# Updates by halves of both token tiles, and first transposes in the tail of the stage before, in a two-block decoder kernel

## What is computed

```python
def first_block(x, ...):
    h = x
    for l in range(DEPTH):
        h = h + 0.5 * swiglu(rmsnorm(h, ffn_pre_norm[l]), ...)
        u = rmsnorm(h, mix_norm[l])
        h = h + (pool_mixer(u, ...) if l < N_A_LAYERS else mla_attention(u, ...))
        h = h + 0.5 * swiglu(rmsnorm(h, ffn_post_norm[l]), ...)
        if l == N_A_LAYERS - 1:
            k_nope, k_rope, v = mla_shared_kv(h, ...)
    return rmsnorm(h, final_norm)

def second_block(x, norm_g, ...):
    h = x
    for l in range(DEPTH):
        g = norm_g[l]
        f = swiglu_2(rms_norm(h, g[0]), ffn1_w_in[l], ffn1_w_out[l])
        h = h + FFN_RES * rms_norm(f, g[1])
        m = even_mixer(rms_norm(h, g[2]), ...) if l % 2 == 0 else odd_mixer(rms_norm(h, g[2]), ...)
        h = h + rms_norm(m, g[3])
        f = swiglu_2(rms_norm(h, g[4]), ffn2_w_in[l], ffn2_w_out[l])
        h = h + FFN_RES * rms_norm(f, g[5])
    return h
```

## Time and profile before

| | us |
|---|---|
| median of 3 runs | 1914.13 (1913.56 to 1914.39) |
| profiled execution | 1913.66 |
| its span, first to last instruction | 1911.9 |
| TensorE busy | 1888.3 (99%) |
| VectorE busy | 1227.6 (64%) |
| ScalarE busy | 945.5 (49%) |
| GpSimd busy | 62.4 (3%) |
| granted TensorE clock, mean | 0.999 |

### The profile page before, as it was taken

One profiled execution on the slowest core, in us unless ns is written; L12 is line 12 of the kernel. 1 busy time (PEld: TensorE's weight loads), 2 busy tenths in 40 slices (PEclk: granted clock), 3 DMA queues, 4 the chain that ended last, 5 costly groups with the idle time before them and its releaser, 6 DMA issues.

```text
span 1911.9 us, 34343 instructions
## 1 busy us (share of the span) xinstructions
PE 1888.3 (99%) x13542; PEld 1755.5 (92%) x13542; DVE 1227.6 (64%) x1645; ACT 945.5 (49%) x1295; POOL 62.4 (3%) x98
## 2 busy tenths in 40 slices
PE   9999999999999999999999999999999999999998
PEld 8999999999998889999999998899999998889997
DVE  6666766675555646665766689666666665876665
ACT  5444544454446645444544458644454446455443
POOL 0000100000001000000100000100000001010000
PEclk9999999999999999999999999999999999999999
DMA  7555355545553145555554442655545553344552
GB/s 284 198 197 198 135 202 197 187 166 201 187 197 130 67 143 189 196 197 198 198 196 185 157 144 96 237 207 192 185 165 201 191 198 124 130 153 168 196 197 99
DMA packets 61361, 338.83 MB, mean 177 GB/s; under 512 B 6960, under 2 KB 7344, under 8 KB 32880
## 3 DMA queue, kind: packets, MB, share of 16 engines
q1 hardware_dynamic: 59328, 330.00, 46.8%
q0 software_dynamic: 1968, 7.93, 1.2%
HBM read 336.85 MB, written 1.05 MB: 177 GB/s over the span
## 4 chain that ended last, share of the span: by engine, by line
PE 92%; DVE 3%; ACT 2%; issue 1%; POOL 1%; DMA 0%; SPq 0%; DVEq 0%; ACTq 0%; POOLq 0%
PE X L1582 56%; PE Y L1582 34%; DVE xl L1084 1%; ACT hiA L563 1%; PE X L1600 1%; DVE loA L1057 0%; ACT xh L609 0%; DVE arena L1370 0%; DMA rawA<-in_wa 0%; PE Y L1979 0%; PE X L1622 0%; PE X L1624 0%; POOL ms_eps L465 0%; POOL rstd L451 0%; DVE xs L1120 0%
## 5 line engine op out<-in xcount | busy, mean ns | idle before, releaser
L1582 PE MATMUL X<-xh,hiA 128*128 128x256 f32 x2592 | 722.4, 279 | 4.6 <-DVE xl L1084 3.0
L1582 PE MATMUL X<-xl,hiA 128*128 128x256 f32 x2592 | 717.6, 277 | 0.0
L1582 PE MATMUL X<-xh,loA 128*128 128x256 f32 x2592 | 717.1, 277 | 0.0
L1057 DVE TENSOR_TENSOR loA<-rawA,hiA 128x2048 fp32r<-128x2048 f32 x220 | 504.0, 2291 | 269.0 <-ACT hiA L563 268.6
L1582 PEld LDWEIGHTS X<-xh,hiA 128*128 128x128 f32 x2592 | 486.8, 188 | 9.1 <-issue 4.7
L1582 PEld LDWEIGHTS X<-xl,hiA 128*128 128x128 f32 x2592 | 487.5, 188 | 0.0
L1582 PEld LDWEIGHTS X<-xh,loA 128*128 128x128 f32 x2592 | 487.2, 188 | 0.0
L563 ACT ACTIVATE hiA<-rawA 128x2048 fp32r<-128x2048 f32 (+1 forms) x234 | 423.7, 1811 | 56.7 <-PE Y L1582 30.5
L1582 PE MATMUL Y<-hiB,act_hl 128*128 128x512 f32 (+1 forms) x880 | 275.8, 346 | 0.0
L1582 PE MATMUL Y<-hiB,act_hh 128*128 128x512 f32 x704 | 275.2, 391 | 0.1
L1582 PE MATMUL Y<-loB,act_hh 128*128 128x512 f32 x704 | 275.0, 391 | 0.0
(11 more groups left out here) (250 smaller groups left out, 2079.7 us busy)
## 6 DMA issues: line engine op xcount, KB each, us to landing
rawA<-in_wa SPq DMA_DIRECT2D x221, 1024.0 KB, 5.4
rawB<-in_wb SPq DMA_DIRECT2D x181, 512.0 KB, 3.5
row_gain<-in_rows POOLq DMA_DIRECT2D x8, 512.0 KB, 6.4
arena<-in_gla POOLq DMA_DIRECT2D x1, 1280.0 KB, 10.2
h<-in_x SPq DMA_DIRECT2D x2, 512.0 KB, 4.0
out<-h SPq DMA_DIRECT2D x2, 512.0 KB, 2.6
arena<-in_pool POOLq DMA_DIRECT2D x1, 768.0 KB, 5.6
arena<-in_taps POOLq DMA_DIRECT2D x1, 576.0 KB, 4.5
```

What stands on the lines that cost most here:

```text
L1057: nc.vector.tensor_tensor(loA[p][:, :], rawA[p][:, :], hiA[p][:, :].bitcast(f32), ALU.subtract).then_inc(a_lo, 1)
L1582: return say(nc.tensor.matmul(*args, **kw))
```

## The change

For the stages behind a second-block update (hyb, ffn5, ffn6, gla, ffn7: `crossed`) the update before them adds both first halves first: (0,0), (1,0), (0,1), (1,1). `wait_h` counts places in that order, and `residual` transposes slots 0 to 2 of both tiles and then slots 3 to 7 of both, by calling `transposes` four times with a range of slots. The last update, ahead of the output, stays tile by tile, with `add(0, 1)` ahead of `weighted(1, 0)`.

For mla and ffn3 (`early`) the transposes of tile 0 are issued by the stage before, ahead of its last quarter (`following`), and only tile 1 is left at the start. As nothing but a `mm` releases the owed weight buffer there, ScalarE of ffn3 splits tile a+1 behind `xt_hi`, in two halves with the square of tile 1 between them and that of tile 0 ahead of `xt_hi`; VectorE follows with `half_A`.

The tail of every feed-forward stage gives (1,0) before it finishes the other tile's product for (1,1). The first projection of mla runs over slots with the `xh` products of both tiles, waiting for `xh_done`, and then the `xl` products. `opened` is False for every stage, so `opening` and `block_late` are not used.

```diff
--- before.py
+++ after.py
@@ -62,7 +62,12 @@
         raw = late or kind in ("mla", "gla")
         mixers = [p["kind"] for p in plan if p["kind"] != "final"]
         ahead = bool(mixers) and mixers[-1] == "ffn"
-        s = dict(at, kind=kind, i=i, name=name, second=second, reuse=reuse, late=late, raw=raw, ahead=ahead)
+        before = plan[-1] if plan else None
+        crossed = bool(before) and before["second"]
+        early = raw and bool(before) and not crossed and before["kind"] in ("ffn", "mla")
+        opened = False
+        s = dict(at, kind=kind, i=i, name=name, second=second, reuse=reuse, late=late, raw=raw, ahead=ahead,
+                 crossed=crossed, early=early, opened=opened)
         pre = 0 if reuse else 2
         mid = {"kv": 2, "mla": 2, "hyb": 2, "gla": 8}.get(kind, 0)
         s["norm_mid"] = at["norm"] + pre
@@ -270,7 +275,7 @@
         ident_loaded, zero_set, gain_loaded = sem("ident_loaded"), sem("zero_set"), sem("gain_loaded")
         phase_loaded = {k: sem(f"{k}_loaded") for k in ("pool", "mla", "hyb", "gla")}
         row_loaded = [sem("row_loaded0"), sem("row_loaded1")]
-        half_set = sem("half_set")
+        half_set, half_hi, half_lo = sem("half_set"), sem("half_hi"), sem("half_lo")
         ms_done, eps_done, rstd_done = sem("ms_done"), sem("eps_done"), sem("rstd_done")
         ln_eps = sem("ln_eps")
         sum_eps = sem("sum_eps")
@@ -365,7 +370,8 @@
             if s["update"] == 0:
                 engine.wait_ge(x_loaded[t], 16)
             else:
-                engine.wait_ge(h_done, 4 * (s["update"] - 1) + 2 * t + half + 1)
+                place = 2 * half + t if s["crossed"] else 2 * t + half
+                engine.wait_ge(h_done, 4 * (s["update"] - 1) + place + 1)
 
         HALF = [slice(0, 512), slice(512, 1024)]
         HEAD_AFTER = (0, 3, 5, 7)
@@ -637,16 +643,27 @@
                     act.wait_ge(gain_loaded, 16)
                 if s["reuse"]:
                     latent_square()
-                if a and not s["ahead"]:
+                def token_square(t):
+                    mean_square(s["norm"] + t, h[:, t, :], xs[:, t, :], D ** -0.5)
+
+                halved = s["early"] and not s["ahead"]
+                if halved:
+                    wait_h(act, s, 0)
+                    token_square(0)
+                elif a and not s["ahead"]:
                     split_A(a + 1, (a + 1) % 2)
                 if not s["reuse"]:
                     xt_hi(s, s["name"])
                 if a == 0:
                     split_A(1, 1, 0).then_inc(head_hi, 1)
                     split_A(1, 1, 1)
-                if s["late"]:
-                    for t in range(TT):
-                        mean_square(s["norm"] + t, h[:, t, :], xs[:, t, :], D ** -0.5)
+                if halved:
+                    split_A(a + 1, (a + 1) % 2, 0).then_inc(half_hi, 1)
+                    token_square(1)
+                    split_A(a + 1, (a + 1) % 2, 1)
+                elif s["late"]:
+                    token_square(0)
+                    token_square(1)
                 split_B(b, b % 2)
 
                 def step(f, p, first=False, last=False):
@@ -1057,6 +1074,11 @@
                 nc.vector.tensor_tensor(loA[p][:, :], rawA[p][:, :], hiA[p][:, :].bitcast(f32),
                                         ALU.subtract).then_inc(a_lo, 1)
 
+            def half_A(n, part, done):
+                p, cut = n % 2, slice(D * part, D * part + D)
+                nc.vector.tensor_tensor(loA[p][:, cut], rawA[p][:, cut], hiA[p][:, cut].bitcast(f32),
+                                        ALU.subtract).then_inc(done, 1)
+
             def split_B(n, p):
                 dve.wait_ge(b_hi, n + 1)
                 nc.vector.tensor_tensor(loB[p][:, :], rawB[p][:, :], hiB[p][:, :].bitcast(f32),
@@ -1130,10 +1152,13 @@
                 weighted(0, 0)
                 weighted(0, 1)
                 add(0, 0)
+                if s is plan[-1]:
+                    add(0, 1)
                 weighted(1, 0)
-                add(0, 1)
                 weighted(1, 1)
                 add(1, 0)
+                if s is not plan[-1]:
+                    add(0, 1)
                 add(1, 1)
 
             def ffn(s):
@@ -1142,7 +1167,18 @@
                     latent_keys()
                 else:
                     xt_lo(s, s["name"])
-                if a == 0:
+                halved = s["early"] and not s["ahead"]
+                if s["opened"]:
+                    add_eps(s["norm"], s["square"] + 1, halves=False)
+                if halved:
+                    dve.wait_ge(half_hi, 1)
+                    half_A(a + 1, 0, half_lo)
+                if s["opened"]:
+                    add_eps(s["norm"] + 1, s["square"] + 2, halves=False)
+                if halved:
+                    dve.wait_ge(a_hi, a + 2)
+                    half_A(a + 1, 1, a_lo)
+                elif a == 0:
                     dve.wait_ge(head_hi, 4)
                     nc.vector.tensor_tensor(loA[1][:, 0:D], rawA[1][:, 0:D], hiA[1][:, 0:D].bitcast(f32), ALU.subtract
                                             ).then_inc(head_lo, 1)
@@ -1153,18 +1189,20 @@
                     split_A(a + 1, (a + 1) % 2)
                 if s["reuse"]:
                     latent_eps(plan[plan.index(s) - 1])
-                if s["late"]:
+                if s["late"] and not s["opened"]:
                     for t in range(TT):
                         add_eps(s["norm"] + t, s["square"] + t + 1, halves=False)
 
                 def step(f, p, first=False, last=False):
                     split_B(b + f, (b + p) % 2)
-                    up = X[:, 2 * p + 1, 0:TOKENS]
+                    gate, up = X[:, 2 * p, 0:TOKENS], X[:, 2 * p + 1, 0:TOKENS]
+                    if first and s["opened"]:
+                        gate, up = Y[:, 2, 0:TOKENS], Y[:, 3, 0:TOKENS]
                     if s["late"]:
                         if first:
                             dve.wait_ge(root_done, s["deferred"] + 1)
                         dve.wait_ge(gate_psum, e + 1 + f)
-                        nc.vector.tensor_tensor(act_s[:, p, :], X[:, 2 * p, 0:TOKENS], root, ALU.mult
+                        nc.vector.tensor_tensor(act_s[:, p, :], gate, root, ALU.mult
                                                 ).then_inc(gate_scaled, 1)
                         dve.wait_ge(up_psum, e + 1 + f)
                         nc.vector.tensor_tensor(act_h[:, p, :], up, root, ALU.mult).then_inc(up_scaled, 1)
@@ -1599,7 +1637,7 @@
                 for _ in range(n):
                     nc.tensor.transpose(dst, ident[:, :], ident[:, :])
 
-            def transposes(s, t):
+            def transposes(s, t, ks=range(KD)):
                 if t == 0 and s["kind"] == "hyb":
                     keep_busy(34)
                 if not s["raw"]:
@@ -1610,7 +1648,7 @@
                     idle = ((6, 7), (5, 2))
                 if s["late"] and before and before["kind"] == "final":
                     idle = ((14, 2), (8, 0))
-                for k in range(KD):
+                for k in ks:
                     dst, src = x_slot(k)[:, P * t:P * t + P], h[:, t, P * k:P * k + P]
                     if k == 3 and s["raw"]:
                         keep_busy(idle[t][1])
@@ -1622,10 +1660,45 @@
                         ins = nc.tensor.transpose(dst, src, ident[:, :])
                     else:
                         ins = nc.tensor.matmul(dst, src, diag(t), start=True, stop=True)
-                    if k == 0:
+                    if k == 0 and t == 0:
                         say(ins)
                     if t == TT - 1:
                         ins.then_inc(xt_psum, 1)
+
+            def residual(s):
+
+                if s["crossed"]:
+                    for ks in (range(0, 3), range(3, KD)):
+                        for t in range(TT):
+                            transposes(s, t, ks)
+                else:
+                    if not s["early"]:
+                        transposes(s, 0)
+                    transposes(s, 1)
+
+            def following(s):
+
+                n = plan.index(s) + 1
+                if n < len(plan) and plan[n]["early"]:
+                    transposes(plan[n], 0)
+
+            def opening(s, out_aps, done):
+
...
+                owed.append(a_free)
 
             def wait_x(s, k=KD - 1):
 
@@ -1717,8 +1790,7 @@
                     ins.then_inc(kv_root, 1)
 
                 if not s["reuse"]:
-                    transposes(s, 0)
-                    transposes(s, 1)
+                    residual(s)
                 if a == 0:
                     keep_busy(12, Y[:, 3, 384:512])
 
@@ -1730,6 +1802,28 @@
                             between()
                         ins = by_weights(X[:, 2 * p + j, 0:TOKENS], wh[:, j, k, :], wl[:, j, k, :], k,
                                          k == 0, k == KD - 1, tokens_h(s), tokens_l(s))
+                    ins.then_inc((gate_psum, up_psum)[j], 1)
+
```

(33 more changed lines are left out.)

33 lines of the change are left out of this document (added).

## The result

| | before | after |
|---|---|---|
| median of 22 runs each | 1913.53 (1912.36 to 1914.83) | 1916.28 (1915.66 to 2139.42) |
| profiled execution | 1913.66 | 1915.89 |
| its span | 1911.9 | 1914.1 |
| GpSimd busy | 62.4 | 59.8 |

The ratio is 1.0015, 95% interval 1.0009 to 1.0021: 2.75 us slower, which is within 0.2% of no change, though the interval lies above 1. (The 2139.42 is one run at a mean clock of 0.828; the others end at 1917.49.) The forecast was 1921.1 with a range from 1917.0: the direction was right, the size was not.

What follows compares the result with a forecast made beforehand. TensorE, 92% of the chain, was taken to bound the kernel, losing time only at hand-overs of h. hyb 4.9, crossed starts 0.9 and mla to ffn3 1.2 sum to +7.0 on 1914.13: 1921.1 us, range 1917.0 to 1926.5.

Steps and rivals of the forecast that it cites:

- the first sentence on hyb: Start of hyb: claimed the tail of transposes is called twice for t=0, issuing 34 filler transposes again, +3.7 us.
- the 4.9 for this place: Start of hyb: whole delay, slot 6 of the first block from 1106.55 to about 1111.5, +4.9 us.
- the fillers: Start of hyb: a second, uncovered set of 34 filler transposes at 0.109 each, +3.7 us.
- the crossed order of the transposes: Start of hyb: slots 0 to 2 of both tiles, then 3 to 7; 0.4 of the 4.9 us.
- late diagonals of hyb: Start of hyb: the new add order delays ScalarE's last square and moves the second diagonal 0.82 us later.
- Crossed starts: Starts of ffn5, ffn6, gla, ffn7: about even, slightly dearer, +0.17, +0.26, +0.46 and 0, together +0.9 us.
- mla to ffn3: Early transposes wait for adds ahead of mla's last quarter, the weight split loses its cover, norms follow: +1.2 us.
- ffn2 to mla: Early transposes and the first projection's new order in mla change nothing: 0, bounds -0.7 and +0.3 us.
- tails: Feed-forward stages give (1,0) 0.68 us earlier, (1,1) unchanged: 0, down to -0.1 each for pool, kv, final.
- last update: Before the output: add (0,1) comes earlier, (1,0) and (1,1) stay, the second output DMA ends last: 0.
- The clock: Rival: the clock falls in hyb, to half under the second fillers and diagonal transposes; 1927 to 1931 us, chance 0.10.
- That hyb gives the delay back: Rival: the hybrid stage absorbs the 4.9 us, +2.1 stays: 1916.2 us, no change by measurement; chance 0.07.
- The crossing pays: Rival: fillers hide, earlier adds gain 0.8, mla gains 0.7, ffn3 loses only 0.4: +3.8, 1917.9 us; chance 0.13.

Runs made afterwards that it cites:

- e1: The changed kernel with hyb made to call residual, so its 34 fillers are issued twice: 1921.02 us, ratio 1.0037 to the kernel before.
- e5: The changed kernel with the old order of adds ahead of hyb: 1915.87 us, ratio 1.0010 to the kernel before.
- e2: e1 with keep_busy(34) only in the first of the four transposes calls, so the fillers are issued once: 1917.14 us, one run.
- e6: The changed kernel without the 7 and 2 fillers between the halves of ffn5, ffn6, gla and ffn7: 1915.47 us, ratio 1.0010 to the kernel before.
- e9: Changed kernel, ffn3 not early, old adds ahead of hyb, no fillers between halves, gla's tile 0 raw squares behind xt_hi: 1913.67 us, ratio 0.9999 to before.
- e3: The changed kernel with no stage early, all transposes at the start of their stage: 1914.75 us, ratio 1.0006 to the kernel before.
- e8: The changed kernel with ffn3 waiting for its split by halves and both add_eps ahead of them: 1915.41 us, ratio 1.0009 to the kernel before.
- e10: The kernel before with only weighted(1,1) put ahead of add(0,1) in the updates: 1916.32 us, one run.

## Why the prediction was right and wrong

**The step that failed** is the first sentence on hyb: "The tail of `transposes` is called twice for t=0". It isn't. `ks` has a default, the diff puts `residual` into ffn, mla and gla only, and `hyb` keeps its two plain calls. I took the plan's `crossed`, which is true for hyb, for a statement on who transposes how; the section on the change says the same of hyb and is wrong there too. For hyb it governs only `wait_h` and, with it, the order in which quarters are waited for. Of the 4.9 for this place 3.7 were the fillers and 0.4 the crossed order of the transposes, neither of which exists in after. Without them the sum of the same working is +2.9; measured are +2.75 by the medians and +2.33 by the marks. e1 puts the call in, and its terms come out one by one: hyb 4.72 for 4.9, the crossed starts 0.73 for 0.9, mla to ffn4 1.01 for 1.2.

**The late diagonals of hyb**: 0.82 forecast, 0.86 in after (0.67 to 0.86 over five kernels), 0.92 by the difference of e5. The reason (three adds in a row, three squares in the old order behind the second of them) stands in the rows. Right. The order of the transposes, put at 0.4, is 0.17 to 0.36 by e2.

**Crossed starts**: 0.17, 0.26 and 0.46 forecast, 0.20, 0.19 and 0.58 in after (0.02 to 0.23, 0.19 to 0.25 and 0.38 to 0.58 over the seven kernels with fillers there). The mechanism at ffn5 and ffn6, the fillers that VectorE's two adds no longer cover, is confirmed by e6; that at gla, the square ahead of `xh`, by e9. ffn7 was put at 0; its step of -0.31 is in the part that I give to no edit.

**mla to ffn3**: 1.2 forecast, 0.91 in after and 1.1 as after against e3. Slot 3 of t=1 at 726.19 was forecast, and is 726.02 in a profile that is 0.2 early there. The split of 1.2 into a late first block and a lost cover is right too; e8 finds 0.7 for the latter.

**ffn2 to mla, tails, last update**: 0 each, and the marks show nothing there that stands out of their scatter of up to 0.18. Right as far as can be told, though the tails may sum to a few tenths of gain.

**The rivals.** The clock stayed 1.00 in hyb in after and in e1, with the second fillers. That hyb gives the delay back was priced at 1916.2, and 1916.28 were measured: a coincidence, for it fell with e1, where the 4.72 are all there at ffn5, with 0.11 more (0.20 more in after). "The crossing pays" names a true effect with the wrong sign in this version: it pays at ffn5 and ffn6 in e6, where the fillers are gone, and not at gla.

## What to carry to other kernels

A helper that gets a new parameter changes nothing for callers that don't pass it: read the call sites in the diff one by one before pricing what the helper does, and put the largest term of a sum on a line of the code, not on a flag's name. Fillers ahead of a wait cost nothing only as long as the wait is longer; when an edit puts the data of the other tile first, their number has to be counted again. And transposes of the next stage can go into a tail only where their input needs nothing from the quarter that they displace; where that held, they still gained nothing that shows (mla), or lost since the adds came late and the work behind them had lost its cover (ffn3).

## What the runs showed of the chip

e10 is 1.13 later from mla to ffn3, at a place that its edit doesn't touch. Windows of its timeline (columns as above), and a stretch of matmuls:

```profile
602.00:604.00 2.00, 1.51 (x7) 1.51 (x8) 1.84 (x4) 1.69 (x1) 0.00 (x0) 0.67 0.08 29
604.00:606.00 2.00, 2.00 (x12) 2.00 (x11) 2.00 (x1) 1.20 (x2) 0.00 (x0) 0.50 0.00 0
```

```profile
603.38 0.41 PE L1582 MATMUL X<-cql,hiA 128*128 128x256 f32 x1
603.59 0.41 PE L1582 MATMUL X<-cqh,loA 128*128 128x256 f32 x1
```

The granted clock went from 2.4 to 1.2 GHz for about 3.5 us, and these matmuls are 0.21 apart. In before, in the same place:

```profile
601.98 0.38 PE L1582 MATMUL X<-cqh,hiA 128*128 128x256 f32 x1 [0.55 <-DVE cql L1282]
```

```profile
602.00:604.00 2.00, 1.94 (x14) 1.74 (x15) 1.84 (x2) 1.97 (x3) 0.00 (x0) 1.00 0.05 14
```

There the matmuls are 0.12 apart. Just ahead of it TensorE stood idle 1.25 and 0.54 us in e10, and 1.26 and 0.55 in before, where the clock held. So the two waits alone don't decide it, and what did no row here shows. In no other profile here is any window of 2 us ahead of 1906 below 0.97. Some timed runs look alike: of 22 runs of after four have a mean clock of 0.998, with a median of 1917.14, against 1916.04 for the fifteen at 0.999. That these have the same cause is inferred from the size (e10's 1.13), not shown. It may be why a profile of one run can be 1 us off a median, and e10's time can't be read as the price of its edit.
